# One product per strip of 32 output columns for the closing sum of an encoder layer

## The reference, cut to what matters

```python
out = lax.map(run_block, (xbuf, block_e)).reshape(n_slots, D)
y = jnp.zeros((T + 1, D), dt).at[slot_tok].add(out * slot_w[:, None].astype(dt))[:T]
...
x = _post_ln(alpha * x + (1.0 + g2[:, None, :]) * y, ln2_g[l], ln2_b[l])
```

## Time and profile before

| | |
|---|---|
| median of 3 runs (lowest, highest) | 1517.87 us (1516.25, 1518.43) |
| profiled execution, its own time | 1519.21 us |
| its span, first to last instruction | 1517.3 us |
| mean granted clock of TensorE | 0.991 of 2.4 GHz |
| TensorE busy, VectorE busy | 1466.9 us (97%), 564.5 us (37%) |
| ScalarE busy, GpSimd busy | 351.8 us (23%), 98.6 us (6%) |
| bytes moved by DMA | 305.49 MB, 201 GB/s over the span |

### The profile page before, as it was taken

The page is one execution under the profiler, slowest core; times in us unless marked ns, Lnnn a source line. Parts: engine busy times, 40 slices in busy tenths (PEclk is TensorE's granted clock), DMA queues, the critical chain, the costliest instruction groups (busy, mean ns, idle before and its releaser), DMA issues. The chain is left out here.

```text
span 1517.3 us, 19808 instructions
## 1 busy us (share of the span) xinstructions
PE 1466.9 (97%) x7315; PEld 808.6 (53%) x7316; DVE 564.5 (37%) x1133; ACT 351.8 (23%) x739; POOL 98.6 (6%) x98
## 2 busy tenths in 40 slices
PE   7999999999989999999999899999999999999997
PEld 4555554447768666665555544444444444444443
DVE  2222117556879443436777700111111111011128
ACT  1112122137734343433111011111111110111111
POOL 0000002000000000000000111111111111111110
PEclk9999999999999999999999899999999999999999
DMA  9401001128840300004111599879789879999965
GB/s 342 165 28 42 0 1 36 45 55 237 265 128 1 118 0 0 0 0 166 60 56 70 222 383 394 321 287 413 314 329 418 320 311 412 425 369 413 424 282 202
DMA packets 101797, 305.49 MB, mean 201 GB/s; under 512 B 18353, under 2 KB 61661, under 8 KB 92536
## 3 DMA queue, kind: packets, MB, share of 16 engines
q1 hardware_dynamic: 93064, 287.08, 49.3%
q0 software_dynamic: 8064, 16.80, 3.0%
q10 hardware_dynamic: 624, 1.03, 0.2%
HBM read 289.86 MB, written 25.76 MB: 208 GB/s over the span
## 5 line engine op out<-in xcount | busy, mean ns | idle before, releaser
L2009 PE MATMUL ps<-w_down_sb,hidT 128*128 x320 | 153.4, 612 | 0.0
L462 PE MATMUL ps<-w_in_tok,uT 128*128 128x512 f32 (+2 forms) x384 | 141.5, 529 | 0.0
L1993 PE MATMUL ps<-w_gate_sb,x_slotsT 128*128 x320 | 140.7, 593 | 0.7 <-ACT x_slotsT L2092 0.7
L1993 PE MATMUL ps<-w_up_sb,x_slotsT 128*128 x320 | 140.6, 592 | 0.0
L1664 PE MATMUL ps<-uT,hT 128*128 128x512 f32 x256 | 112.9, 594 | 0.3 <-ACT hT L1604 0.3
L632 PE MATMUL ps<-uT,mod 128*128 128x512 f32 x256 | 111.0, 593 | 0.8 <-PEq L218 0.8
L2248 DVE TENSOR_TENSOR hid<-silu_g,ps 128x512 f32<-128x512 f32 x20 | 13.7, 687 | 258.5 <-PE ps L1993 258.5
L462 PEld LDWEIGHTS ps<-w_in_tok,uT 128*128 128x128 f32 x384 | 72.6, 190 | 65.5 <-issue 43.9
L1993 PEld LDWEIGHTS ps<-w_gate_sb,x_slotsT 128*128 128x128 f32 x320 | 60.7, 190 | 76.9 <-issue 76.9
L1993 PEld LDWEIGHTS ps<-w_up_sb,x_slotsT 128*128 128x128 f32 x320 | 60.8, 190 | 76.5 <-issue 76.5
L2009 PEld LDWEIGHTS ps<-w_down_sb,hidT 128*128 128x128 f32 x320 | 55.8, 189 | 65.1 <-issue 64.3
(11 more groups left out here) (431 smaller groups left out, 1892.9 us busy)
## 6 DMA issues: line engine op xcount, KB each, us to landing
light_gate_sb<-in_w_gate SPq DMA_DIRECT2D x20, 2048.0 KB
light_up_sb<-in_w_up SPq DMA_DIRECT2D x20, 2048.0 KB
light_down_sb<-in_w_down SPq DMA_DIRECT2D x20, 2048.0 KB
w_gate_sb<-in_w_gate SPq DMA_DIRECT2D x12, 2048.0 KB
w_up_sb<-in_w_up SPq DMA_DIRECT2D x12, 2048.0 KB, 17.9
w_down_sb<-in_w_down SPq DMA_DIRECT2D x12, 2048.0 KB, 23.2
mod<-in_w_ada SPq DMA_DIRECT2D x8, 1024.0 KB, 9.0
w_ada_late<-in_w_ada SPq DMA_DIRECT2D x8, 1024.0 KB, 7.2
```

Of the source, the lines that this page charges most:

```text
L462: mm = nc.tensor.matmul(ps[:, 2 + g, 0:n], self.uT[:, k, t * P:(t + 1) * P], wt[:, k, c0:c0 + n], start=k == 0, stop=k == KD - 1)
L1993: m = m_.matmul(ps[:, bank, :], xT[:, k, :], wt[:, bass.ds(buf, 1), k, :].rearrange("p a f -> p (a f)"), start=k == 0, stop=k == KD - 1)
L2009: m = m_.matmul(ps[:, 5 + half, :], hT[:, k, :], wd[:, bass.ds(buf, 1), k, half * 512:half * 512 + 512].rearrange("p a f -> p (a f)"), sta ...
```

## The change

In the last stage the eight tiles are cut into four strips (s) of 32 tokens. For each strip, 96 partitions hold three stacked blocks: the first expert's rows of the 32 tokens (partitions 0 to 31), the second expert's rows (32 to 63), and the x1 rows (64 to 95); the four strips of a tile lie side by side in the free dimension. One product with three stacked 32x32 diagonals (w0, w1, alpha) gives the sum of a strip and one half of the columns, and the four strips of a tile go to the four strips of 32 output columns.

- Loads: a pair load becomes two loads of 512 KB, k = 0 and k = 1, into 32 partitions each, in pieces of 4 KB; x1 goes to 32 partitions as well. Tiles 0 to 6 have rooms of their own (gate, gate, up, up, light gate, light up, light down weights) and their x1 loads wait for the last product that uses that room. Tile 7 uses tile 0's room again and waits for its sum.
- TensorE: `residual` and `rows_of_experts` become `rows_of_tile`; ahead of tile 0 stand eight products of `keep_clocked`.
- Diagonals: VectorE makes all of them once, ahead of the block loop; ScalarE's go.
- Epsilon is added in the square root, a copy takes the place of the addition, and the reciprocal stands ahead of the wait for L2273's result.

```diff
@@ -1779,8 +1779,9 @@
         s_x1 = [self.sem(f"x1_loaded{t}") for t in range(TT)]
         s_y = [self.sem(f"pair_loaded{t}") for t in range(TT)]
         s_cv, s_var, s_std, s_o, s_st = (self.sem(n) for n in ("cb_dve", "varC", "stdC", "out_ready", "out_stored"))
-        s_al, s_dg, s_sum, s_read = self.sem("alpha_diagonal"), self.sem("weight_diagonals"), self.sem("rows_summed"), self.sem("sum_read")
-        yb = self.ybuf.rearrange("(t p k) d -> t p k d", p=P, k=2)
+        s_dg, s_sum, s_read = self.sem("weight_diagonals"), self.sem("rows_summed"), self.sem("sum_read")
+        yb = self.ybuf.rearrange("(t s p k) d -> t k p s d", s=4, p=LC, k=2)
+        x1b = self.x1d.rearrange("(t s p) d -> t p s d", s=4, p=LC)
         SUM_BANKS = (0, 2, 6, 4)
         with ExitStack() as x, nc.Block() as block:
             sb = lambda n, s, dt=F32: self.sb(n, s, dt, ctx=x)
@@ -1825,13 +1826,15 @@
             pos = sb("pos", [P, 2, TT])
             cmp_ = sb("cmp", [P, 5, E])
             col = sb("table_cols", [P, 5])
-            al, dg = sb("alpha_diag", [P, P]), sb("weight_diag", [P, 2, 2, P])
-            st, mv, ve = sb("stC", [P, 2, 6]), sb("mvC", [P, 2]), sb("veC", [P, 2, 2])
-            x1 = wg[:].rearrange("p a k f -> p (a k f)").rearrange("p (t d) -> p t d", t=TT)
+            w3, i3, dg = sb("weights_by_strip", [P, TT, 4]), sb("three_identities", [P, LC]), sb("weight_diag", [P, TT * 4, LC])
+            var, std = sb("row_variance", [P, TT]), sb("std_or_inverse", [P, TT])
+            eps = sb("ln_eps", [P, 1])
+            st, mv = sb("stC", [P, 2, 6]), sb("mvC", [P, 2])
             z = wd[:].rearrange("p a k d -> p (a k) d")
-            pairs = [buf.rearrange("p (t k d) -> p t k d", k=2, d=D) for buf in (
-                wu[:].rearrange("p a k f -> p (a k f)"), lwg[:].rearrange("p k f -> p (k f)"), lwu[:].rearrange("p k f -> p (k f)"))]
-            yt = lambda t: pairs[0][:, t] if t < 4 else pairs[t // 2 - 1][:, t % 2]
+            strips = lambda buf: buf.rearrange("p (s d) -> p s d", s=4)
+            homes = [strips(buf[:, j].rearrange("p k f -> p (k f)")) for buf in (wg, wu) for j in range(2)]
+            homes += [strips(buf[:].rearrange("p k f -> p (k f)")) for buf in (lwg, lwu, lwd)]
+            rows3 = lambda t: homes[t % len(homes)]
             sums = lambda t, half: ps[:, SUM_BANKS[t % 4] + half, :]
             s_used = (s_G, s_U, s_Y)
             count = lambda eng: eng.value_load(tbl[0:1, 4, 0:1], min_val=1, max_val=NB - 1)
@@ -1868,13 +1871,17 @@
                             sp.dma_start(dst[:, bass.ds(buf, 1)].rearrange("p a k f -> p (a k) f"),
                                          src[bass.ds(e, 1)].rearrange("a p k f -> p (a k) f")).then_inc(s_w[j], 16)
 
-                sp.wait_ge(s_G, n + 1)
-                for t in range(TT):
-                    sp.dma_start(x1[:, t], self.x1d[t * P:(t + 1) * P, :]).then_inc(s_x1[t], 16)
-                sp.wait_ge(s_yfree, n + 1)
-                sp.wait_ge(s_lyfree, n + 1)
-                for t in range(TT):
-                    sp.dma_start(yt(t), yb[t]).then_inc(s_y[t], 16)
+                for t, (s_free, freed) in enumerate(((s_G, n + 1), (s_G, n + 1), (s_U, n + 1), (s_U, n + 1), (s_lG, n + 1), (s_lG, n + 1), (s_lY, n + 1), (s_sum, 1))):
+                    if t == TT - 1:
+                        sp.wait_ge(s_yfree, n + 1)
+                        sp.wait_ge(s_lyfree, n + 1)
+                        for u in range(t):
+                            for k in range(2):
+                                sp.dma_start(rows3(u)[k * LC:(k + 1) * LC], yb[u, k]).then_inc(s_y[u], 16)
+                    sp.wait_ge(s_free, freed)
+                    sp.dma_start(rows3(t)[2 * LC:3 * LC], x1b[t]).then_inc(s_x1[t], 16)
+                for k in range(2):
+                    sp.dma_start(rows3(TT - 1)[k * LC:(k + 1) * LC], yb[TT - 1, k]).then_inc(s_y[TT - 1], 16)
                 for t in range(TT):
                     sp.wait_ge(s_o, t + 1)
                     sp.dma_start(self.out[t * P:(t + 1) * P, :], z[:, t]).then_inc(s_st, 16)
@@ -2045,42 +2052,32 @@
                     m.then_inc(s_lY, 1)
                     down(1, range(KF // 2, KF)).then_inc(s_Y, 1)
 
-                def residual(t):
+                def rows_of_tile(t):
                     if t > 3:
                         pe.wait_ge(s_read, t - 3)
                     pe.wait_ge(s_x1[t], 16)
+                    pe.wait_ge(s_y[t], 32)
                     for half in range(2):
-                        m_.matmul(sums(t, half), al[:], x1[:, t, half * 512:half * 512 + 512], start=True, stop=False)
-
-                def rows_of_experts(t):
-                    pe.wait_ge(s_y[t], 16)
-                    pe.wait_ge(s_dg, 2 * t + 2)
-                    for k in range(2):
-                        for half in range(2):
-                            m = m_.matmul(sums(t, half), dg[:, t % 2, k, :], yt(t)[:, k, half * 512:half * 512 + 512], start=False, stop=k == 1)
+                        for s in range(4):
+                            m = m_.matmul(ps[s * LC:(s + 1) * LC, SUM_BANKS[t % 4] + half, :], dg[0:3 * LC, 4 * t + s, :],
+                                          rows3(t)[0:3 * LC, s, half * 512:half * 512 + 512], start=True, stop=True)
                     m.then_inc(s_sum, 1)
 
-                pe.wait_ge(s_al, 1)
+                pe.wait_ge(s_dg, 1)
                 pe.wait_ge(s_xT, n + 1)
                 pe.wait_ge(s_lxT, n + 1)
-                residual(0)
                 pe.wait_ge(s_sg, n + 1)
                 pe.wait_ge(s_h, n + 1)
-                residual(1)
                 pe.wait_ge(s_lh, n + 1)
                 pe.wait_ge(s_yd, n + 1)
-                residual(2)
                 pe.wait_ge(s_lyd, n + 1)
+                self.keep_clocked(4, 8)
                 for t in range(TT):
-                    rows_of_experts(t)
-                    if t + 3 < TT:
-                        residual(t + 3)
+                    rows_of_tile(t)
 
             @block.scalar
             def _(act):
                 a = nc.scalar
-                ident = self.c(C_ID)
-                a.mul(al[:], ident, ALPHA).then_inc(s_al, 1)
                 act.wait_ge(s_d, 1)
                 a.activation(gx[:, 1], gx[:, 1], ACT.Exp).then_inc(s_e, 1)
                 act.wait_ge(s_d2, 1)
@@ -2104,18 +2101,9 @@
                     act.wait_ge(s_lxt, b + 2)
                     a.copy(xlT[:].rearrange("p k t -> p (k t)"), ps[:, 0, 0:KD * LC]).then_inc(s_lxT, 1)
 
-                def diagonals(t):
-                    if t > 1:
-                        act.wait_ge(s_sum, t - 1)
-                    for k in range(2):
-                        a.mul(dg[:, t % 2, k, :], ident, self.wts[:, k, t:t + 1]).then_inc(s_dg, 1)
-
-                diagonals(0)
                 for t in range(TT):
-                    if t + 1 < TT:
-                        diagonals(t + 1)
                     act.wait_ge(s_var, t + 1)
-                    a.activation(ve[:, t % 2, 1:2], ve[:, t % 2, 0:1], ACT.Sqrt).then_inc(s_std, 1)
+                    a.activation(std[:, t:t + 1], var[:, t:t + 1], ACT.Sqrt, bias=eps[:]).then_inc(s_std, 1)
 
             @block.vector
             def _(dve):
@@ -2241,6 +2229,17 @@
                 for q in range(4):
                     v.tensor_copy(gate2q[q * LC:(q + 1) * LC, :], self.gate2[q * LC:(q + 1) * LC, q * Q:(q + 1) * Q]).then_inc(s_gq, 1)
                 dve.wait_ge(s_gq, 4)
+                v.memset(eps[:], LN_EPS).then_inc(s_gq, 1)
+                v.memset(w3[2 * LC:3 * LC], ALPHA).then_inc(s_gq, 1)
+                for k in range(2):
+                    for s in range(4):
+                        v.tensor_copy(w3[k * LC:(k + 1) * LC, :, s], self.wts[s * LC:(s + 1) * LC, k, :]).then_inc(s_gq, 1)
+                for k in range(3):
+                    part = slice(k * LC, (k + 1) * LC)
+                    v.tensor_copy(i3[part], self.cst[part, C_ID + k * LC:C_ID + (k + 1) * LC]).then_inc(s_gq, 1)
+                dve.wait_ge(s_gq, 17)
+                v.tensor_tensor(dg[0:3 * LC], i3[0:3 * LC].unsqueeze(1).to_broadcast([3 * LC, 4 * TT, LC]),
+                                w3[0:3 * LC].rearrange("p t s -> p (t s)").unsqueeze(2).to_broadcast([3 * LC, 4 * TT, LC]), ALU.mult).then_inc(s_dg, 1)
                 with turns(dve, n) as b:
                     dve.wait_ge(s_U, b + 2)
                     dve.wait_ge(s_sg, b + 2)
@@ -2263,18 +2262,18 @@
                 cb = Chain(dve, s_cv)
                 dve.wait_ge(self.s_again, 32)
                 for t in range(TT):
-                    j, bank = t % 2, SUM_BANKS[t % 4]
+                    bank = SUM_BANKS[t % 4]
                     rows = ps[:, bank:bank + 2, :].rearrange("p a b -> p (a b)")
                     dve.wait_ge(s_sum, t + 1)
                     cb.link(v.bn_stats(st[:, 0, :], sums(t, 0)))
                     cb.link(v.bn_stats(st[:, 1, :], sums(t, 1)))
```

(8 more changed lines are left out.)

## The result

The changed kernel took 1526.13 us (median of six runs, 1523.1 to 1528.43) beside 1518.55 us for the kernel before (six runs): a ratio of 1.0045, 95% interval 1.0032 to 1.0058. By the ratio it is slower by about 6.8 us; the two medians lie 7.6 us apart, and the new one is 0.1 us above the upper end of the forecast's range (1526). Its profiled execution took 1526.86 us, span 1525.0 us, mean granted clock 0.977 (0.991 before).

A forecast was written before the change was run, and what follows sets the result against it. The prediction took TensorE to bind the old last stage and half-rate loads the new one: 17 loads to 1511.0, then sum, VectorE and store to 1520.7, 3.4 us later than before, so 1521.3 on the median; range 1513.5 to 1526.

The forecast's parts named there:

- Loads set the pace, at half rate: Last stage: loads into 32 partitions move at 211 GB/s, 4.97 us a tile against VectorE's 4.38; chance 0.65.
- half the partitions take the stream: Pair loads: two slices of 32 partitions are in the queue together, so half of 422 GB/s, 211, was taken.
- 0 to 0.9 us, I take 0.4: Before the pair loads: the last scatter shares the engines with the last x1 load and is delayed by this much.
- The clock: Tile 7's sum: if TensorE falls to 1.2 GHz between loads, 1.9 us more, giving 1523.2; otherwise full clock.
- The sum: End of the kernel: 17 loads until 1511.0, then 0.1, 2.13, 4.44 and 3.03 us, span end 1520.7.
- the case that scatter, clock and load rate all came out badly: Half rate's upper end, 1526: low clock 1.9, full scatter collision 0.5, loads 5% slower 2.1 us.
- The filler: Eight products ahead of tile 0, ending at 1473.1; they delay tile 0 only with full-rate loads (1513.9, chance 0.27).
- 4.38 us a tile without idle: VectorE in the last stage: an earlier reciprocal saves 0.11 us of today's 4.49 us a tile.
- Strips side by side: TensorE's sums: four strips run together, sixteen passes in 1.86 us; if not, 6.88 us a tile, 1536.4, chance 0.04.
- Stores: Kernel end: seven stores queued behind pair 7 finish at about 1519 and hold the last store by 0 to 0.5 us.

The follow-up runs named there:

- the run with ranges: Kernel before, with pair loads queued by partition range (whole, 0 to 63 and 64 to 127, 32 to 95, 0 to 31 and 96 to 127): 1520.91 us in one execution.
- The three runs on the filler: Changed kernel with filler products also between the sums (three each: 1.0044; five behind tile 6: 1.0055), or without any filler (1.0050); ratios to the kernel before.
- the filled runs: Changed kernel with twelve filler products ahead of tile 0 and three behind each later sum (1.0044), or five behind tile 6 (1.0055); ratios to the kernel before.

## Why the prediction was right, point by point

- **Loads set the pace, at half rate.** Right: 203 to 211 GB/s against the 211 taken, pairs 5.05 us apart against 4.97, and 37.60 us from tile 0's sum to tile 7's against 42.2 - 4.97 = 37.2. The reason given (half the partitions take the stream) was a guess from rows, and it isn't quite the reason: in the run with ranges 64 partitions moved at 420 GB/s in one place and at 224 in another, and loads of 32 at 230. The place of the 64 is what halved the rate; the forecast's number was right because 0 to 63 is such a place. By its own reason it would have given half rate to 32 to 95 as well, so to that extent the number was luck. The Trainium skill ("SBUF — State Buffer", section on the DMA port swizzle) has just this: bit 6 of the partition number picks one half of the ports. By that rule 32 to 95 reaches all of them, and this case's 420 GB/s agrees; the 137 GB/s of the x1 loads doesn't follow from it. The Trainium skill's 189 to 196 GB/s at 1 MiB is a little under the 203 to 230 seen here.
- **The scatter, mis-sized.** The step "0 to 0.9 us, I take 0.4" failed. The scatter took 6.66 us, 3.5 more than before. The mechanism was named, but its price came from the leftover of one load, with x1 in by 1464.9. x1's last load landed at 1467.5, and the scatter 1 us behind it; the run with a quarter of x1 gave the time back. The three runs on the filler have the same program up to here, and their scatters took 5.3, 6.4 and 5.1 us, each landing about 1 us behind the last x1 load (1466.2, 1467.0 and 1465.9). So the term is 1.9 to 3.5 us, and it goes by when x1 is through. Why a scatter of 3.2 us cannot finish beside the loads stays open.
- **The clock, taken at the wrong end.** The sum took 1.2 GHz as the less likely case. The sums ran at 1.2 GHz from tile 1 on, which cost 3.70 instead of 2.13 us from the last sum's start to VectorE's, shown by the filled runs in the profile.
- **The sum.** From the last block's end to the end of the span I had 1520.7 - 1461.3 = 59.4 us. The trace has 64.7 (1460.27 to 1525.0): 3.0 for the later pair issue, 1.6 for the clock, 0.35 for pair 0's landing, 0.4 for the pace. The last stretch before was 56.0 us, so 3.4 us more were forecast and 8.7 came; the timed runs show 6.8. Both mis-sized terms, scatter and clock, went the same way, and the time came out at the upper end of the range, which the forecast had kept for the case that scatter, clock and load rate all came out badly.
- **The filler** was said to end at 1473.1 and to bind only at full rate: right on both (1472.2 with a block loop that ended 1.0 us sooner; no change in the runs without it).
- **VectorE.** It has 13 small instructions more ahead of the block loop, not 14, and they were hidden (15.42 us of idle left there). Where the prediction says that tile 6 follows tile 7, it is tile 7 that follows. 4.38 us a tile without idle was 4.35 in the runs where nothing held it. **Strips side by side** with 96 rows: sixteen passes in 1.92 us.
- **Stores** behind the loads were not the bound, as said.

## What to carry to other kernels

In these runs a load's rate went by which partitions it filled, not by how many (32, 64 or 128) or by its pieces (4 or 8 KB): before stacking operands on a part of the partitions, work out the loads by that rate, and if only 64 can be used, take 64 that straddle the middle, as 32 to 95 do here. A product that makes TensorE cheaper is worth, for each tile, at most the distance to the next bound (here 0.66 us), plus what it takes off the first sum. A slower layout of its inputs can cost more than that, also in transfers of another queue that must land behind them.

## What the runs showed of the hardware that I had not expected

- A load into 32 to 95 moves at 420 GB/s, one into 0 to 63 at 224.
- Loads can hold up another queue's transfer until they are nearly through. The scatter took 3.2 us alone and 5.1 to 6.7 us behind x1 loads in 64 to 95. It took 10.4 and 10.5 us where x1 had crawled at 137 GB/s before and more of it was still to come; by the time the scatter was issued those loads moved at about 200 GB/s as well. In all six of these profiles it landed within 1.1 us of the last x1 load.
- Loads into partitions below 64 ran at 137 GB/s, well under half rate, for some 12 us beside the last block's work, in three kernels.
- The clock stayed at 0.50 from tile 1 to tile 7 of the changed kernel, while TensorE was busy 3.64 of every 5.05 us. That is no rule: without the filler, at the same pace, it was back at 1.00 for tile 4 (1.92 us) and at 0.50 again behind the 3.15 us of idle that followed.
- The clock was at 0.50 after only 2.39 us of idle (three filler products per tile); with idle gaps of 0.3 to 0.7 us it stayed at 1.00, and so it did with gaps of 0.5 to 1.6 us in the run with full-rate pairs and a quarter of x1.
